# The decays of a state-space scan: GpSimd forms the clamped exponents, ScalarE takes the exponential

## What is computed

```python
log_a = dt * a                                     # per token and head, 32 heads, chunks of 128 tokens
a_cum = jnp.cumsum(log_a, axis=-1)
seg = a_cum[..., :, None] - a_cum[..., None, :]
decay_in = jnp.exp(jnp.where(causal, seg, -jnp.inf))
cb = jnp.einsum("bclgn,bcsgn->bcgls", cc, bc)
y_diag = jnp.einsum("bcgjls,bcsgjp->bclgjp", cb[:, :, :, None] * decay_in, x_)
...
y = (y_diag + y_off).reshape(b, s, h, p) + d_skip[:, None] * xh
yf = y * silu(z)                                   # four groups of 512 features
yf = yf * lax.rsqrt(jnp.mean(yf * yf, axis=-1, keepdims=True) + EPS)
```

## Time and profile before

| what | value |
|---|---|
| median of 3 runs | 1694.12 us (1694.06 to 1698.26) |
| profiled execution | 1696.35 us, span 1694.6 us |
| TensorE busy | 1650.3 us, 97% |
| VectorE busy | 676.0 us, 40% |
| ScalarE busy | 580.5 us, 34% |
| GpSimd busy | 43.1 us, 3% |

### The profile page before, as it was taken

The page is one execution under the profiler, slowest core; times in us unless marked ns, Lnnn a source line. Parts: engine busy times, 40 slices in busy tenths (PEclk is TensorE's granted clock), DMA queues, the critical chain, the costliest instruction groups (busy, mean ns, idle before and its releaser), DMA issues.

```text
span 1694.6 us, 23925 instructions
## 1 busy us (share of the span) xinstructions
PE 1650.3 (97%) x9885; PEld 1047.6 (62%) x9885; DVE 676.0 (40%) x1194; ACT 580.5 (34%) x819; POOL 43.1 (3%) x26
## 2 busy tenths in 40 slices
PE   9999999989999999999999999999999999999998
PEld 8999853333333333333333333349999989999997
DVE  4776641212121212121212121244597665666654
ACT  5655321111111111111111111144464797466433
POOL 0000000000000000000000000000100032000000
PEclk9999999999999999999999999999999999999999
DMA  8556899999999999999999999985556654555552
GB/s 268 200 199 225 301 418 422 416 412 429 430 430 429 431 428 432 429 432 429 431 430 430 429 429 428 431 311 177 177 178 223 187 175 130 175 186 180 188 190 87
DMA packets 153392, 539.38 MB, mean 318 GB/s; under 512 B 8210, under 2 KB 102862, under 8 KB 120430
## 3 DMA queue, kind: packets, MB, share of 16 engines
q1 hardware_dynamic: 150974, 534.20, 80.1%
q10 hardware_dynamic: 2352, 4.23, 0.8%
HBM read 537.33 MB, written 1.08 MB: 318 GB/s over the span
## 4 chain that ended last, share of the span: by engine, by line
PE 63%; DMA 12%; DVE 2%; ACT 2%; issue 1%; SPq 0%
PE bank L1463 17%; PE bank L169 10%; PE bank L171 9%; PE bank L170 9%; PE bank L1499 9%; DMA expert_weights<-in_expert_w_up_dram 6%; DMA expert_weights_late<-in_expert_w_up_dram 6%; PE bank L1443 2%; PE bank L1424 2%; PE bank L1484 2%; PE bank L1432 1%; ACT back_w_hi L113 1%; DVE back_w_lo L117 0%; PE bank L1437 0%; PE bank L2093 0%
## 5 line engine op out<-in xcount | busy, mean ns | idle before, releaser
L1361 DVE TENSOR_TENSOR pre_act<-bank,bias_now 128x512 f32<-128x512 f32 x64 | 44.0, 687 | 652.1 <-PE bank L1484 652.1
L117 DVE TENSOR_TENSOR back_w_lo<-raw_weights,back_w_hi 128x2048 fp32r<-128x2048 f32 x90 | 205.5, 2286 | 91.7 <-ACT back_w_hi L113 90.7
L1463 PE MATMUL bank<-expert_weights_late,x_gathered 128*64 128x512 f32 x1008 | 222.7, 593 | 11.3 <-DMA expert_weights_late<-in_expert_w_up_dram 11.3
L169 PE MATMUL bank<-u_hi,back_w_hi 128*128 128x256 f32 x704 | 201.2, 286 | 0.2 <-DVE u_lo L1900 0.2
L113 ACT ACTIVATE back_w_hi<-raw_weights 128x2048 fp32r<-128x2048 f32 x90 | 170.1, 1891 | 89.6 <-PE bank L171 89.6
L170 PE MATMUL bank<-u_lo,back_w_hi 128*128 128x256 f32 x704 | 199.1, 283 | 0.0
L171 PE MATMUL bank<-u_hi,back_w_lo 128*128 128x256 f32 x704 | 199.1, 283 | 0.0
L1463 PE MATMUL bank<-expert_weights,x_gathered 128*64 128x512 f32 x752 | 166.8, 593 | 8.5 <-DMA expert_weights<-in_expert_w_up_dram 8.5
L1463 PEld LDWEIGHTS bank<-expert_weights_late,x_gathered 128*64 128x64 f32 x1008 | 71.2, 137 | 159.3 <-issue 135.1
L1282 ACT ACTIVATE pre_act<-bank 128x512 f32<-128x512 f32 x32 | 19.1, 597 | 396.0 <-PE bank L1463 383.7
L169 PEld LDWEIGHTS bank<-u_hi,back_w_hi 128*128 128x128 f32 x704 | 134.9, 192 | 2.8 <-issue 2.6
(11 more groups left out here) (420 smaller groups left out, 2643.2 us busy)
## 6 DMA issues: line engine op xcount, KB each, us to landing
expert_weights_late<-in_expert_w_up_dram SPq DMA_DIRECT2D x63, 2048.0 KB, 24.4
expert_weights<-in_expert_w_up_dram SPq DMA_DIRECT2D x47, 2048.0 KB, 25.3
expert_weights_late<-in_expert_w_down_dram SPq DMA_DIRECT2D x31, 2048.0 KB, 28.8
raw_weights<-in_w_in_dram SPq DMA_DIRECT2D x56, 1024.0 KB, 5.4
expert_weights<-in_expert_w_down_dram SPq DMA_DIRECT2D x22, 2048.0 KB, 28.0
raw_weights<-in_expert_w_up_dram SPq DMA_DIRECT2D x15, 2048.0 KB, 23.8
raw_weights<-in_w_up_dram SPq DMA_DIRECT2D x22, 1024.0 KB, 5.1
raw_weights<-in_expert_w_down_dram SPq DMA_DIRECT2D x8, 2048.0 KB, 27.3
```

Of the source, the lines that this page charges most:

```text
L117: dve.tensor_tensor(self.w_lo[:, s, 0:size], self.s.raw[:, s, 0:size], self.w_hi[:, s, 0:size].bitcast(FP32), ALU.subtract).then_inc(self. ...
L169: pe.matmul(out, lhsT=ah, rhs=bh, start=start, stop=False, skip_group_check=shared)
L1361: dve.tensor_tensor(both.rearrange("p g k n -> p (g k) n").rearrange("p a (h n) -> p a h n", h=2), TB[b][:, :].rearrange("p (a h n) -> p a ...
L1463: m = pe.matmul(U[b][rows[half], :], lhsT=xg[:, 2 * u + a, :], rhs=w[:, a, 512 * c:512 * c + 512], start=(first and a == 0), stop=(last an ...
```

## The change

GpSimd forms the exponents: for each pair, six instructions of 128x128 subtract the shift from the running sum and take the minimum with zero. ScalarE keeps only the `exp` over 128x768. `decays` on ScalarE now waits for the six instructions; the waits for the loaded sums and for `scan_out(p-2)` move to GpSimd. GpSimd's list, which had only the gate, the adding of squares and the norm of each group, is written out anew: the work on pair p comes first, the gates of groups 0, 1, 2 stand behind the exponents of pairs 6, 9 and 13, the adding of squares behind those of pairs 7, 10 and 14, the norms behind those of pairs 8, 11 and 15. Pairs 0 and 1 wait only for the shift, the sums and the tile to be free.

```diff
+            def decay_args(p):
+                pool.wait_ge(shift_ready, 1)
+                pool.wait_ge(sums_loaded[p % (ROWS // 2)], 16 * (p // (ROWS // 2) + 1))
+                if p >= 2:
+                    pool.wait_ge(y_mm, p - 1)
+                else:
+                    pool.wait_ge(xtok_ready, 1)
+                    pool.wait_ge(ya_done, 4)
+                for hh in range(2):
+                    h, row = 2 * p + hh, sums[:, (2 * p + hh) % ROWS, :]
+                    for b, c in ((0, slice(0, P)), (1, slice(P, T)), (2, slice(P, T))):
+                        pool.tensor_scalar(decay[:, p % 2, hh, P * b:P * b + P], row[:, c], shift[:, b, h:h + 1], 0.0,
+                                           op0=ALU.subtract, op1=ALU.min).then_inc(args_ready, 1)
...
+            for p in range(N_HEADS // 2):
+                decay_args(p)
+                for g, at in ((0, 6), (1, 9), (2, 13)):
+                    if p == at:
+                        gate_group(g)
+                for g, at in ((0, 7), (1, 10), (2, 14)):
+                    if p == at:
+                        add_squares(g)
+                    if p == at + 1:
+                        norm_group(g)
+            gate_group(3)
+            norm_group(3)
...
             def decays(p):
 
-                act.wait_ge(sums_loaded[p % (ROWS // 2)], 16 * (p // (ROWS // 2) + 1))
-                if p >= 2:
-                    act.wait_ge(y_mm, p - 1)
-                for hh in range(2):
-                    h, row = 2 * p + hh, sums[:, (2 * p + hh) % ROWS, :]
-                    for b, c in ((0, slice(0, P)), (1, slice(P, T)), (2, slice(P, T))):
-                        own.add(act.activation(decay[:, p % 2, hh, P * b:P * b + P], row[:, c], ACT.Relu, scale=-1.0,
-                                               bias=shift[:, b, h:h + 1]))
-                own.wait()
+                act.wait_ge(args_ready, 6 * (p + 1))
                 both = decay[:, p % 2, :, :].rearrange("p h b -> p (h b)")
-                act.activation(both, both, ACT.Exp, scale=-1.0).then_inc(decay_ready, 1)
+                act.activation(both, both, ACT.Exp).then_inc(decay_ready, 1)
```

More of the change, by code:

```diff
@@ L1658, in mixer2 @@
         w_dt_split, dt_heads_mm, dt_copied = sem("m3_w_dt_split"), sem("m3_dt_heads_mm"), sem("m3_dt_copied")
-        squares_added = sem("m3_squares_added")
+        squares_added, args_ready = sem("m3_squares_added"), sem("m3_args_ready")
         sums_stored = sem("m3_sums_stored")
@@ L1730, in gpsimd, with gate_group @@
                 pool.tensor_tensor(pair(bcv, j), pair(bcv, j), pair(bcv, 8 + j), ALU.mult).then_inc(ya_ready, 1)
-            for g in range(N_GROUPS):
+            def decay_args(p):
[11 more added lines that the diff above has]
+                                           op0=ALU.subtract, op1=ALU.min).then_inc(args_ready, 1)
+            def gate_group(g):
                 y = xbc[:, 4 * g:4 * g + 4, :].rearrange("p a t -> p (a t)")
@@ L1737, in gpsimd, with add_squares, norm_group @@
                 pool.tensor_tensor(y, y, zt[:, 4 * g:4 * g + 4, :].rearrange("p a t -> p (a t)"), ALU.mult).then_inc(gated, 1)
-                if g < N_GROUPS - 1:
-                    pool.wait_ge(squared, 2 * g + 2)
-                    pool.tensor_tensor(squares[0], squares[0], squares[1], ALU.add).then_inc(squares_added, 1)
+            def add_squares(g):
+                pool.wait_ge(squared, 2 * g + 2)
+                pool.tensor_tensor(squares[0], squares[0], squares[1], ALU.add).then_inc(squares_added, 1)
+            def norm_group(g):
                 pool.wait_ge(rstd_ready, g + 1)
```

## The result

The changed kernel takes 1732.91 us (median of 5 runs, 1730.99 to 1734.87) against 1694.12 us: a ratio of 1.0222, 95% interval 1.021 to 1.0233, or 38.8 us more. The direction was forecast, the size was not: I had summed 17 us. 1732.9 lies outside the chain's own range (1704 to 1718) and inside the stated one, where the rival of dearer GpSimd instructions stood (1723 to 1737).

A forecast was written before the change was run, and what follows sets the result against it. TensorE, busy 1650.3 of 1694.6 us, was taken to bound the kernel. Group delays of 8.8 + 5.3 + 3.45 - 0.5 = 17 us on the 1694.12 us median gave 1711 us, range 1698 to 1735.

The forecast's parts named there:

- the chain's own range: Delays summed through GpSimd's list, ScalarE and VectorE in the scan: 1704 to 1718 us, chance 0.60.
- the rival of dearer GpSimd instructions: New GpSimd instructions cost more than its two-input ones, 0.6 to 0.8 us: 1723 to 1737 us, chance 0.17.
- What bounds: Whole scan: TensorE bounds; its three waits for weighted decays, 1.9 us in all, are all any relief can win.
- What goes: ScalarE loses 96 Relus, six a pair at 1.85 us; in an ordinary round that wins nothing.
- What comes: 96 GpSimd instructions of 128x128, each taken at t = 0.31 us, 1.85 us a pair.
- the upper bound: Price of one new GpSimd instruction from above: 0.475 us for 128, worked out from larger two-input rows.
- 17 + 42 (t - 0.31): Scan's total loss in us for instruction time t, 42 instructions on the chain: 10 at 0.14 to 24 at 0.475.
- Two engines, one port: GpSimd and VectorE instructions on two SBUF tensors exclude each other; the new instructions were assumed to take turns too.
- Ordinary rounds: Rounds without gate, adding or norm: VectorE loses at most 0.62 of 1.05 us; cost nothing up to t = 0.53.
- The rival's term, 2t - 1.05: Dearer instructions: what each ordinary round adds past t = 0.53, ten rounds of 0.55 us at t = 0.8.
- GpSimd's order: Gate, adding and norm stand before later pairs' exponents: groups cost 8.8, 5.3 and 3.45 us, less 0.5.
- A to D: First group: TensorE delayed 0.3, 1.6, 1.55 and 5.3 us at `scan_out(6)`, the mean of squares, `scan_out(8)` and `scan_out(9)`.

The follow-up runs named there:

- the late low parts: Kernel before the change, with VectorE making the first two normed groups' low parts one unit later: 1693.68 us, ratio 0.9987.
- the two halves: Changed kernel with GpSimd preparing only pairs 0 to 6, 10, 13 (1707.5 us), or only the other seven (1729.29 us); ScalarE does the remaining Relus.
- the kernel that prepares ahead: Changed kernel with a third half of the decay tile, pairs prepared one round earlier, gates, addings and norms one pair later: 1708.78 us, ratio 1.0074.
- three two-input: Changed kernel with three two-input GpSimd subtractions a pair instead of six instructions, no minimum, exponential of a hundredth: 1708.97 us, ratio 1.0075.
- the filled kernel: Changed kernel with unread TensorE matmuls in front of the first mean of squares and the scans of pairs 9, 11, 12, 15: 1731.3 us, ratio 1.0207.

## Why the prediction was right in direction and wrong in size

*What bounds.* Right: 1.9 us were to be won, and the late low parts won about that by a reordering.

*What goes.* Right: ScalarE lost its 96 Relus, and no round got shorter by it.

*What comes.* This is the step that failed: "One tensor read and one written lies between ... so I take the middle, t = 0.31 us". I ranked the forms by the tensors they read and gave their arithmetic no price. A copy, with the same one read and one write, does take 0.29 us; the `tensor_scalar` took 0.71, above the two-input 0.45, so the upper bound was no bound. In the prediction's own sum, 17 + 42 (t - 0.31), 0.71 gives 34 us: the chain was right, and this term was sized at less than half. The rival of dearer instructions bracketed the time, with a chance of 0.17; its reason, reading the shift, is only 0.08 us of the 0.40 too little. No row of that form existed, and its chance should have been larger.

*Two engines, one port.* Half right. The gate still stops `lo` (3.58 us at 1360.01). But the new instructions and VectorE do not take turns evenly. In an ordinary round of the changed kernel, VectorE and GpSimd:

```profile
1323.30 2.29 DVE L117 TENSOR_TENSOR back_w_lo<-raw_weights,back_w_hi 128x2048 fp32r<-128x2048 f32 x1 [1.34 <-ACT back_w_hi L113]
1325.51 0.95 DVE L1999 TENSOR_TENSOR b_c_v<-b_c_v,x_b_c 128x768 f32<-128x768 f32 x1
...
1322.26 1.41 POOL L1744 TENSOR_SCALAR b_c_v<-decay_sums,decay_shift 128x128 f32<-128x128 f32 x2 [1.76 <-PE bank L2117]
1323.64 3.32 POOL L1744 TENSOR_SCALAR b_c_v<-decay_sums,decay_shift 128x128 f32<-128x128 f32 x1
```

*Ordinary rounds.* "Cost nothing, up to t = 0.53" was not tried at its edge. At 0.71, TensorE waits 0.42 and 0.72 us at the scans of pairs 2 and 5, by GpSimd's lateness at `exp`, not by VectorE's turns. The rival's term, 2t - 1.05 in each of ten rounds, is 3.7 us at 0.71 and would bring the sum to 37.5; that this is the measured loss is luck, since the ordinary rounds did not cost that much. That GpSimd itself would be full (six of 0.71 and the 2.6 us in which `lo` and m hold it, against a round of 6.75) was a limit that I had not looked for.

*GpSimd's order.* Right in place, and shown by the two halves and by the kernel that prepares ahead. The longest waits came at `scan_out(9)` and `scan_out(12)`, 7.35 and 5.84 us. The starts of the scans show it group by group; `scan_out(12)` and `scan_out(15)` before, then `scan_out(5)`, `scan_out(12)` and `scan_out(15)` in the changed kernel:

```profile
1404.79 0.66 PE L2093 MATMUL bank<-b_c_v 128*64 128x256 f32 x4
1426.49 0.66 PE L2093 MATMUL bank<-b_c_v 128*64 128x256 f32 x4
...
1356.36 0.66 PE L2116 MATMUL bank<-b_c_v 128*64 128x256 f32 x4 [0.72 <-DVE b_c_v L1999]
1434.03 1.13 PE L2116 MATMUL bank<-b_c_v 128*64 128x256 f32 x4 [5.84 <-DVE b_c_v L1999]
1462.10 1.13 PE L2116 MATMUL bank<-b_c_v 128*64 128x256 f32 x4 [3.32 <-DVE b_c_v L1999]
```

| from, to | the sum at t = 0.71, us | the change, us longer than before | the sum at a set of 1.76 | three two-input, us longer than before |
|---|---|---|---|---|
| `scan_out(5)` to `scan_out(9)` | 15.95 | 15.95 | 8.45 | 7.48 |
| `scan_out(9)` to `scan_out(12)` | 10.1 | 10.96 | 5.1 | 3.17 |
| `scan_out(12)` to `scan_out(15)` | 8.25 | 6.37 | 3.25 | 1.35 |

(In the kernel with three two-input instructions the four scans start at 1354.17, 1389.80, 1415.58 and 1438.63.) With the price put right, the first group is as summed. Step by step, A to D carried through at 0.71 give waits of 0.7, 3.6, 3.95 and 7.7 us, against 1.33, 3.75, 1.04 and 7.35; the 1.04 is 3.32 in the filled kernel, where the clock stays up, so steps B to D agree within 0.7 us, and the agreement of the sum to the hundredth is luck. The second group costs more than its sum in the changed kernel, and less with the cheaper sets; a piece that I called harmless is the set of pair 10 behind the second gate, with 1.15 us at `scan_out(10)`. The third group costs less in both.

*The clock* was in no step. It fell in the waits, and the filled kernel shows that this did not add to the time as far as it was tested.

## What to carry to other kernels

An upper bound taken from a "heavier" form of another operation is no bound; where no row shows the form, a probe of it, or a wide range, comes first. When work moves to an idle engine, read its whole instruction list: each old step that now stands in front of a step on the path is a wait on both engines, and six short instructions a round can fill an engine that the page shows at 3%. What a relief can win is the bounding engine's wait in that stage, here 1.9 us.

## What the runs showed of the hardware

- GpSimd's `tensor_scalar` (float32, value per partition, two operations) takes 0.71 us for 128 and 1.14 for 256 elements; a two-input instruction takes 0.45 and 0.61, a copy of 128 takes 0.29.
- Two VectorE instructions on two SBUF tensors, back to back, stretched one such GpSimd instruction to 3.32 us and took their usual 2.29 and 0.95 us themselves; a two-input GpSimd instruction of 2.41 us did hold VectorE's (3.58 us in place of 2.29).
- TensorE's granted clock, 1.00 before, was 0.58 over the 7 us around the end of a 7.35 us wait, and filling that wait with matmuls brought it back to 1.00 without making the kernel measurably faster.
